# Token gate values computed behind the first expert step's activation, and the gate rows' difference taken by GpSimd

## The chip, the core and the metric

The kernel runs on one core of one Trainium2 chip. The core has TensorE (PE, matrix products and transposes), VectorE (DVE), ScalarE (ACT), GpSimd (POOL) and SyncE (SP, which here only starts transfers), each with an instruction list of its own; they meet through semaphores. 16 DMA engines serve all of the core's transfers. The metric is the device time of one execution in microseconds (us), the median of several.

## What is computed

Two layers of a backbone for 128 context tokens and 512 latent tokens of width 1024. Each layer normalises and modulates the rows, mixes them (pooling and attention), adds the result through a gate, and then runs a grouped mixture of 16 experts with two chosen for each token. The part that matters here, cut from the reference:

```python
def moe(h, router_w, router_b, w_gate, w_up, w_down):
    scores = jax.nn.sigmoid(t @ router_w)
    ...                                      # best group, then the top 2 in it: idx
    wts = jnp.take_along_axis(scores, idx, axis=-1)
    wts = wts / jnp.sum(wts, axis=-1, keepdims=True)
    gates = sum over the two of one_hot(idx) * wts
    act = jax.nn.silu(t @ w_gate) * (t @ w_up) * gates
    return act @ w_down

def trunk_layer(...):
    ...
    x = x + gate2 * moe(h2, ...)
```

`gates` are the token gates: two numbers for each token. `gate2` is a row of 1024 numbers, one row for context tokens and one for latent tokens.

## The kernel before

The kernel is written by hand in the order of each engine's list: one block of code per engine, no scheduler. Each engine runs its list in order; a wait holds all that stands behind it on that engine.

The expert stage of a layer works in steps of 128 gathered rows (`step(n, ...)` in the blocks of PE, ACT and DVE). Tokens are sorted by expert and padded to pieces of 32, so a step holds four tiles of 32 rows, of one to four experts. In this run the first layer has 12 steps and the second 13, numbered from 0. A step on PE (`products`, L1166) multiplies the rows by w_gate and w_up, in four pieces of weights; then `rest` turns the next step's rows (L1132), turns the activation (`turn_act`, L1176) and multiplies by w_down (L1193). In every step but the first of a layer, PE reads the weights of one tile from the ring directly, and ACT (L1499) and DVE (L2291) copy the weights of two others, six pieces a step, into buffers of their own (`part_copy_w`). DVE also multiplies the activation (L2335, two halves), copies half of the turned rows (L2240, `rows_copy`), makes the selected row of gate2 for each slot (L2346 and L2348, which read `is_ctx` and the difference of the two gate rows) and scales the step's output (L2361). ACT stores that output to `y_rows` in memory and then goes on to its next weight piece; the next step but one reads the buffer, so DVE waits for the store (`b_st`). All tensors that are views of one large buffer are called `big` or `actT` in the profile.

Ahead of the first step DVE works through the router: masks, sorted places, the list of rows for the gathers, the tables `fin` (how many steps until an expert is done), `eland` and `eslot` (which weights a tile needs). `r_fin` and `r_slot` tell the other engines that these are ready (L2253 and L2272). Then come the token gates (L2293 to L2304, ten instructions with a wait between most), and `r_gate` after them. The gates' result, `gates2`, is read first in step 2 (`early_gates`). In step 0, DVE takes the difference of the two gate rows (L2343), which L2348 reads in every step.

GpSimd issues the gathers of rows (L1681): the first and the second ahead of step 0, the others one by one as PE has turned the rows before (`b_t`). Each reads its list of rows from `idx`.

SP loads the experts' weights, three transfers of 1 MB each, into a ring of five buffers; `load_expert(e)` waits until the same part of expert e-1 has landed, and from expert 5 on until the buffer's last user is through. The router's scratch lies in the buffer that expert 3 gets. So SP holds the load of expert 3, and all behind it:

```python
                sp.wait_ge(r_gate, L(r_gate) + 1)
                sp.wait_ge(r_slot, L(r_slot) + 1)
                load_expert(3)
                load_expert(4)
```

Of the kernel before, what the change touches and what calls it, by code (L numbers as in the profile page):

```python
# [21 lines left out]
ALU = mybir.AluOpType  # L22
ACT = mybir.ActivationFunctionType
AX = mybir.AxisListType
# [129 lines left out]
def step_kernel(nc, x_prompt, x_sample, cache_ckv, cache_krope, c, c_ctx, ada_w, ada_b, norm1_g, norm2_g, w_in, pool_w,  # L154
# [3 lines left out]
    with es:  # L158
# [275 lines left out]
        def lsem(name, count):  # L434
# [29 lines left out]
        r_mask, r_tot, r_slot, r_fin = (lsem(n, 1) for n in (  # L464
            "r_mask", "r_tot", "r_slot", "r_fin"))
        c_x = lsem("c_x", NT)

        by_layer = [[sem(f"{n}{l}") for n in ("b_t", "b_ta", "b_td", "b_sil", "b_act", "b_at", "b_atc", "b_sel", "b_yd",
                                              "used", "b_st", "b_end", "w_a", "w_d")]
# [1086 lines left out]
        def _(pool):  # L1556
# [4 lines left out]
            for l in range(DEPTH):  # L1561
# [127 lines left out]
                gather(1)  # L1689
                pool.wait_ge(r_fin, L(r_fin) + 1)  # L1690
# [39 lines left out]
        def _(ve):  # L1730
# [69 lines left out]
            for l in range(DEPTH):  # L1800
# [492 lines left out]
                link(tt(gts, sig.rearrange("p (t g) k -> p t (g k)", g=EG), mask16[:, :, :], ALU.mult))  # L2293
                link(red(den, gts, AX.X, ALU.add))
                link(v.reciprocal(den, den))
                link(tt(gts, gts, bc(den, NE), ALU.mult))
                for w in range(2):
                    m = tt(hot[:, w], slot1, bc(pick[:, w, :], NE), ALU.is_equal)
                link(m)
                for w in range(2):  # L2300
                    m = tt(prod[:, w], hot[:, w], gts, ALU.mult)
                link(m)
                for w in range(2):
                    m = red(gates2[:, w * NT:(w + 1) * NT], prod[:, w], AX.X, ALU.add)  # L2304
                link(m)

                ve.sem_inc(r_gate, 1)
# [15 lines left out]
                def step(n, part, last):  # L2323
# [9 lines left out]
                    for k in range(2):  # L2333
                        cols = slice(k * P, (k + 1) * P)
                        v.tensor_tensor(act_n[:, cols], sil[:, cols], tb5[:, cols], ALU.mult).then_inc(b_act, 1)  # L2335
                    if not last:
                        rows_copy(n + 2)
                        if not part:
                            following = part_place(n + 1)
                        part_copy_w(n + 1, following, 0)  # L2340
                        if isinstance(n, int) and n == 0:
                            ve.wait_ge(ld_gate, 64 * l + 64)
                            link(tt(gate[:, 0, :], gate[:, 0, :], gate[:, 1, :], ALU.subtract))  # L2343
# [64 lines left out]
```

## Time and profile before

| | us |
|---|---|
| median of 3 runs | 1065.38 |
| lowest, highest | 1063.85, 1067.24 |
| the profiled execution | 1071.81 |
| its span | 1070.0 |

The profile is of one execution. A page gives each engine's busy time, 40 slices of the span (each digit is a busy share in tenths), and groups of instructions. Answers on the trace give instructions in order of time: start in us, duration in us (for several, from the first's start to the last's end), engine, line of the kernel, what is written and read, and in brackets the idle time before it on its engine with what ended that idle time. The first layer's expert stage runs from about 383 to 531 us, the second's from about 884 to 1050 us. Times in the text are counted from the span's start.

### The profile page before, as it was taken

What the parts mean: (1) busy time and instruction counts of PE and PEld (TensorE: products, weight loads), DVE (VectorE), ACT (ScalarE), POOL (GpSimd) and SP (SyncE); (2) the same over time, 40 slices, a digit from 0 to 9 for tenths busy, and PEclk for the clock granted to TensorE, in tenths of its full rate; (3) what the DMA queues carried; (4) which work ended last, traced back from release to release, by engine and by line L of the source; (5) the groups of instructions that cost most, each with busy time, mean ns of one, the idle gap of its engine ahead of it and who ended that gap; (6) DMA issues with size and microseconds to landing.
All of it is one profiled execution on the core that took longest, in us unless ns stands there. A gap on an engine that the chain in (4) does not pass through costs nothing.

```text
span 1070.0 us, 20675 instructions
## 1 busy us (share of the span) xinstructions
PE 1016.7 (95%) x7322; PEld 551.9 (52%) x7323; DVE 622.8 (58%) x1318; ACT 399.8 (37%) x810; POOL 205.9 (19%) x309
## 2 busy tenths in 40 slices
PE   3999999999999889999989999999999988999987
PEld 1566555555544454555456665555654435555442
DVE  0335455656535886666574545576734687776557
ACT  0332224444311126666433222444521114666550
POOL 0124358000000010010152435800000001000021
PEclk9999999999999999999999999999999999999998
DMA  9960005786800569999980000477250068999936
GB/s 349 373 181 1 1 0 205 276 310 248 332 21 38 197 270 408 419 419 417 374 297 6 1 0 1 185 290 284 86 212 20 40 221 357 420 418 417 411 136 252
DMA packets 71619, 237.90 MB, mean 222 GB/s; under 512 B 12192, under 2 KB 27568, under 8 KB 57216
## 3 DMA queue, kind: packets, MB, share of 16 engines
q1 hardware_dynamic: 59600, 195.36, 47.6%
q0 software_dynamic: 6480, 23.60, 6.0%
q10 hardware_dynamic: 5472, 18.12, 4.2%
q8 instruction: 34, 0.56, 0.2%
q14 instruction: 33, 0.27, 0.1%
HBM read 211.53 MB, written 25.53 MB: 222 GB/s over the span
## 4 chain that ended last, share of the span: by engine, by line
PE 81%; DVE 6%; DMA 5%; issue 3%; POOL 1%; SPq 1%; another core or an unknown queue 1%; ACT 1%; DVEq 0%; ACTq 0%; POOLq 0%
PE pair L1084 13%; PE bank L1166 13%; PE pair L801 8%; PE pair L1193 7%; PE pair L816 6%; PE pair L934 5%; PE bank L711 4%; PE pair L833 4%; PE bank L850 4%; PE bank L970 3%; PE bank L949 3%; DMA big<-ada_w 2%; PE pair L1132 2%; PE bank L785 2%; DMA y_rows<-big 1%
## 5 line engine op out<-in xcount | busy, mean ns | idle before, releaser
L1166 PE MATMUL bank<-big,actT 128*32 (+2 forms) x1168 | 178.6, 379 | 4.1 <-DVE big L2291 2.2
L1499 ACT ACTIVATE actT<-big 128x1024 f32 x138 | 144.3, 1055 | 71.7 <-PE bank L1166 27.0
L1166 PE MATMUL bank<-actT 128*32 128x256 f32 x1840 | 164.7, 379 | 0.0
L1084 PE MATMUL pair<-big,actT 128*128 128x512 f32 x320 | 142.7, 598 | 0.0
L1166 PEld LDWEIGHTS bank<-big,actT 128*32 128x32 f32 (+1 forms) x1168 | 98.9, 114 | 82.0 <-issue 23.7
L801 PE MATMUL pair<-big,actT 128*128 128x384 f32 (+1 forms) x320 | 95.1, 453 | 0.2 <-ACT actT L1256 0.2
L1084 PEld LDWEIGHTS pair<-big,actT 128*128 128x128 f32 x320 | 59.0, 190 | 67.8 <-issue 67.6
L1193 PE MATMUL pair<-big 128*32 (+2 forms) x384 | 92.9, 606 | 0.7 <-ACT big L1514 0.4
L2022 DVE TENSOR_REDUCE mx<-pair 128x1 f32<-128x640 f32 x64 | 52.7, 823 | 65.1 <-PE pair L935 65.0
L1166 PEld LDWEIGHTS bank<-actT 128*32 128x32 f32 x1840 | 86.3, 110 | 0.0
L1193 PE MATMUL pair<-actT,big 128*32 128x512 f32 x368 | 85.3, 607 | 0.0
L2291 DVE COPY big<-big 128x1024 f32 x92 | 63.5, 690 | 35.2 <-PE bank L1166 29.0
L1681 POOL DMA_INDIRECT big<-h_rows,big x25 | 29.8, 1190 | 259.3 <-PE pair L1132 226.9
L801 PEld LDWEIGHTS pair<-big,actT 128*128 128x128 f32 x320 | 60.6, 193 | 29.4 <-ACT actT L1256 1.7
L934 PE MATMUL pair<-big 96*128 96x512 f32 x128 | 70.7, 634 | 1.1 <-PE bank L711 0.9
L816 PE MATMUL pair<-actT,big 128*128 128x512 f32 (+1 forms) x256 | 70.9, 434 | 0.0
L1670 POOL TENSOR_SCALAR ss<-big 128x1 f32<-128x1 f32 x10 | 3.0, 302 | 339.0 <-ACT big L1441 339.0
L711 PE MATMUL bank<-big,condT 128*32 128x512 f32 x384 | 55.0, 657 | 13.6 <-DMA big<-ada_w 13.6
L1383 ACT ACTIVATE big<-pair,nmax 128x640 f32<-128x640 f32 x64 | 50.9, 795 | 18.9 <-DVE nmax L2025 18.5
L1441 ACT ACTIVATE big<-x 128x512 f32<-128x512 f32 x20 | 12.6, 630 | 115.9 <-DVE x L2162 115.9
L816 PEld LDWEIGHTS pair<-actT,big 128*128 128x128 f32 x256 | 39.1, 191 | 29.7 <-issue 29.7
L1193 PEld LDWEIGHTS pair<-big 128*32 128x32 f32 (+1 forms) x384 | 24.8, 114 | 50.5 <-issue 50.4
(303 smaller groups left out, 1627.8 us busy)
## 6 DMA issues: line engine op xcount, KB each, us to landing
big<-ada_w SPq DMA_DIRECT2D x48, 1024.0 KB, 6.3
big<-w_gate SPq DMA_DIRECT2D x32, 1024.0 KB
big<-w_up SPq DMA_DIRECT2D x32, 1024.0 KB
big<-w_down SPq DMA_DIRECT2D x32, 1024.0 KB
y_rows<-big ACTq DMA_DIRECT2D x24, 512.0 KB, 7.5
big<-w_out SPq DMA_DIRECT2D x4, 2048.0 KB, 10.1
big<-mod_rows SPq DMA_DIRECT2D x16, 512.0 KB, 7.0
h_rows<-big ACTq DMA_DIRECT2D x10, 512.0 KB, 2.7
```

The costliest lines, as they stand in the source:

```text
L711: m = mm(a7[32 * j:32 * j + 32, :], condT[:, k, :], w[:, j, :], start=(k == 0), stop=(k == DC - 1), tile_position=(0, 32 * j), skip_group_ ...
L801: m = mm(in_bank(t)[:, to:to + n], actT[:, k, t * P:(t + 1) * P], vw.win_q[:, k, lo:lo + n], start=(k == 0), stop=(k == DC - 1))
L816: m = mm(pair[0][:, to:to + cols], vw.win_p[:, k, g * P:(g + 1) * P], actT[:, k, t0:t0 + cols], start=(k == 0), stop=(k == DC - 1))
L833: m = mm(pair[1][:, n * HALF:n * HALF + 4 * QH], cqT[t % 2][:, k, :], vw.wuq[:, k, n * 4 * QH:(n + 1) * 4 * QH], start=(k == 0), stop=(k = ...
L934: mm(dst[:, 0:HALF], q, vw.kT[0:QH, h, 0:HALF], start=True, stop=True)
L1084: m = mm(dst, actT[:, k, t * P:(t + 1) * P], vw.wo[n][:, k, :], start=(k == order[0]), stop=(k == order[-1]))
L1166: m = mm(dst[lo:lo + m_, 0:DE], xgT[:, k, lo:lo + m_], weights(c, k % 4 * DE, DE), start=(k == 0), stop=(k == DC - 1), tile_position=(0, l ...
L1193: m = mm(pair[1][lo:lo + m_, j * HALF:(j + 1) * HALF], acT[:, k, lo:lo + m_], weights(c, j * HALF, HALF), start=(k == 0), stop=(k == 1), t ...
L1383: f(prob[un % 4][:, :, :], score_bank(un)[:, 0:NLK * P].rearrange("p (k n) -> p k n", n=P), ACT.Exp, bias=nmax[:, un % 2:un % 2 + 1], scal ...
L1499: f(parts[1][i % 3], slot[:, i * PIECE:(i + 1) * PIECE], ACT.Copy).then_inc(w_a, 1)
L2022: link(v.tensor_reduce(mx[:, un % 2:un % 2 + 1], score_bank(un)[:, 0:NLK * P], AX.X, ALU.max))
L2291: v.tensor_copy(parts[2][i % 3], slot[:, i * PIECE:(i + 1) * PIECE]).then_inc(w_d, 1)
```

## The change

The token gates become a function, `token_gates`, that DVE calls in step 0, behind the two activation products and ahead of the copy of the turned rows; before, they stood ahead of step 0. With them goes the signal `r_gate`. The difference of the gate rows is computed by GpSimd, between the second gather and the wait for `r_fin`, and signalled by a new semaphore `g_diff`, on which DVE waits in step 0 at the place where it computed the difference. The last layer's `b_end`, which nobody uses, is not made.

```diff
@@ GpSimd
                 gather(1)
+                pool.wait_ge(ld_gate, 64 * l + 64)
+                tt(gate[:, 0, :], gate[:, 0, :], gate[:, 1, :], ALU.subtract).then_inc(g_diff, 1)
                 pool.wait_ge(r_fin, L(r_fin) + 1)
@@ DVE
-                link(tt(gts, sig.rearrange("p (t g) k -> p t (g k)", g=EG), mask16[:, :, :], ALU.mult))
...
-                link(m)
-
-                ve.sem_inc(r_gate, 1)
+                def token_gates():
+
+                    link(tt(gts, sig.rearrange("p (t g) k -> p t (g k)", g=EG), mask16[:, :, :], ALU.mult))
...
+                    link(m)
+                    ve.sem_inc(r_gate, 1)
+
@@ DVE, step(n, part, last)
                         v.tensor_tensor(act_n[:, cols], sil[:, cols], tb5[:, cols], ALU.mult).then_inc(b_act, 1)
+                    if isinstance(n, int) and n == 0:
+                        token_gates()
                     if not last:
                         rows_copy(n + 2)
                         if not part:
                             following = part_place(n + 1)
                         part_copy_w(n + 1, following, 0)
                         if isinstance(n, int) and n == 0:
-                            ve.wait_ge(ld_gate, 64 * l + 64)
-                            link(tt(gate[:, 0, :], gate[:, 0, :], gate[:, 1, :], ALU.subtract))
+                            ve.wait_ge(g_diff, L(g_diff) + 1)
```

On DVE, at the end of the first layer's router and the start of step 0, the list before (lines L2293 to L2304 are the token gates, L2335 the activation products; a name in brackets is a semaphore that the instruction waits for):

```order
467 L2272 TENSOR_SCALAR big<-big 128x57 [waits dve_chain]
468 L2293 TENSOR_TENSOR big<-big,mask 128x80 [waits r_fin,r_slot]
469 L2294 TENSOR_REDUCE big<-big 128x5 [waits dve_chain]
470 L2295 RECIPROCAL big<-big 128x5 [waits dve_chain]
471 L2296 TENSOR_TENSOR big<-big 128x80 [waits dve_chain]
472 L2298 TENSOR_TENSOR big<-big 128x80 [waits dve_chain]
473 L2298 TENSOR_TENSOR big<-big 128x80
474 L2301 TENSOR_TENSOR big<-big 128x80 [waits dve_chain]
475 L2301 TENSOR_TENSOR big<-big 128x80
476 L2304 TENSOR_REDUCE gates<-big 128x5 [waits dve_chain]
477 L2304 TENSOR_REDUCE gates<-big 128x5
478 L2335 TENSOR_TENSOR big<-big,bank 128x128 [waits dve_chain,used0,b_sil0]
```

The same place on DVE after the change (L2339 is the activation product, L2297 to L2308 the gates, L2242 the copy of the turned rows):

```order
467 L2274 TENSOR_SCALAR big<-big 128x57 [waits dve_chain]
468 L2339 TENSOR_TENSOR big<-big,bank 128x128 [waits b_sil0,used0,r_fin,r_slot]
469 L2339 TENSOR_TENSOR big<-big,bank 128x128
470 L2297 TENSOR_TENSOR big<-big,mask 128x80
471 L2298 TENSOR_REDUCE big<-big 128x5 [waits dve_chain]
...
478 L2308 TENSOR_REDUCE gates<-big 128x5 [waits dve_chain]
479 L2308 TENSOR_REDUCE gates<-big 128x5
480 L2242 COPY actT<-pair 128x512 [waits dve_chain,b_t0]
```

The gates have moved behind both activation products, and so behind what these wait for: PE's products (`used0`) and ACT (`b_sil0`).

On GpSimd, around the second gather (the DMA rows; `TENSOR_LOAD fin` reads the number of steps), before:

```order
136 L1681 DMA big<-h_rows,big 128x1024 [waits r_idx,h_st1,h_st0]
137 L1681 DMA big<-h_rows,big 128x1024 [waits b_t0,r_idx]
138 L1691 TENSOR_LOAD fin [waits r_fin]
139 L1691 ISA x2
140 L1681 DMA big<-h_rows,big 128x1024 [waits b_t0] x8
```

and after:

```order
136 L1681 DMA big<-h_rows,big 128x1024 [waits r_idx,h_st1,h_st0]
137 L1681 DMA big<-h_rows,big 128x1024 [waits b_t0,r_idx]
138 L1691 TENSOR_TENSOR big<-big 128x1024 [waits ld_gate]
139 L1693 TENSOR_LOAD fin [waits r_fin]
140 L1693 ISA x2
141 L1681 DMA big<-h_rows,big 128x1024 [waits b_t0] x8
```

One operation on 1024 columns is added behind the second gather's issue. SP's list is the same before and after; expert 3's first load is the one that waits for `r_gate`:

```order
64 L639 DMA big<-w_down 128x2x1024 [waits ld_wd]
65 L629 DMA big<-w_gate 128x2048 [waits r_slot,ld_wg,r_gate,op_x]
66 L634 DMA big<-w_up 128x2048 [waits ld_wu]
67 L639 DMA big<-w_down 128x2x1024 [waits ld_wd]
68 L629 DMA big<-w_gate 128x2048 [waits ld_wg]
```

Nothing moved in it; what it waits for is now signalled from another place in DVE's list.

## Rows read from the trace of the kernel before

**Rows 1.** The page: busy time by engine, and DMA's busy share in 40 slices.

```profile
PE 1016.7 (95%) x7322; PEld 551.9 (52%) x7323; DVE 622.8 (58%) x1318; ACT 399.8 (37%) x810; POOL 205.9 (19%) x309
...
DMA  9960005786800569999980000477250068999936
```

**Rows 2.** DVE in order of time, first layer: start, duration, line, [idle before it].

```profile
386.50 0.17 DVE L2248 TENSOR_SCALAR fin<-big 128x16 int32<-128x16 f32 x1
...
387.09 0.18 DVE L2253 TENSOR_TENSOR actT<-actT 128x19 f32<-128x19 f32 x1
...
389.97 0.24 DVE L2293 TENSOR_TENSOR big<-big,mask 128x80 f32<-128x80 f32 x1
...
391.88 0.38 DVE L2304 TENSOR_REDUCE gates<-big 128x5 f32<-128x80 f32 x2
392.48 0.49 DVE L2335 TENSOR_TENSOR big<-big,bank 128x128 f32<-128x128 f32 x2 [0.23 <-DVE gates L2304]
393.85 0.69 DVE L2240 COPY actT<-pair 128x512 f32<-128x512 f32 x1 [0.88 <-PE pair L1132]
...
396.21 1.22 DVE L2343 TENSOR_TENSOR big<-big 128x1024 f32<-128x1024 f32 x1
```

**Rows 3.** PE in order of time, at the stages' starts and in step 10.

```profile
383.61 7.14 PE L1166 MATMUL bank<-big,actT 128*128 128x256 f32 x32 [0.36 <-issue]
392.25 0.55 PE L1132 MATMUL pair<-cst,big 128*128 128x128 f32 x3 [1.50 <-DMA big<-h_rows,big]
...
399.79 0.40 PE L1166 MATMUL bank<-big,actT 128*32 x1 [0.64 <-DVE big L2291]
...
511.97 0.39 PE L1166 MATMUL bank<-actT 128*32 128x256 f32 x3
...
893.46 0.33 PE L1176 MATMUL bank<-cst,big 128*128 128x128 f32 x1 [0.72 <-DVE big L2335]
...
900.49 0.40 PE L1166 MATMUL bank<-big,actT 128*32 x1 [0.71 <-DVE big L2291]
...
1013.24 0.40 PE L1166 MATMUL bank<-big,actT 128*32 x1 [0.70 <-ACT actT L1499]
```

**Rows 4.** SP's queue in order of time: loads of w_gate.

```profile
392.38 0.33 SPq L629 DMA_DIRECT2D big<-w_gate  x1
...
504.56 0.33 SPq L629 DMA_DIRECT2D big<-w_gate  x1
...
893.04 0.33 SPq L629 DMA_DIRECT2D big<-w_gate  x1
```

**Rows 5.** Stretches: engines' busy us, PE clock, DMA share, GB/s at the end.

```profile
392.00:393.00 1.00, 0.72 (x5) 0.48 (x6) 0.74 (x4) 0.00 (x0) 0.00 (x0) 1.00 0.00 0
410.00:450.00 40.00, 39.19 (x574) 20.36 (x574) 28.88 (x52) 25.00 (x32) 3.52 (x3) 1.00 1.02 419
```

**Rows 6.** DVE and ACT in order of time: weight copies around step 10.

```profile
504.72 0.69 DVE L2291 COPY actT<-big 128x1024 f32 x1 [0.59 <-DMA big<-w_gate]
...
1005.94 0.69 DVE L2291 COPY actT<-big 128x1024 f32 x1 [2.01 <-DMA big<-w_gate]
...
510.74 1.06 ACT L1499 ACTIVATE actT<-big 128x1024 f32 x1 [2.55 <-PE bank L1166]
...
1012.04 1.06 ACT L1499 ACTIVATE actT<-big 128x1024 f32 x1 [4.05 <-issue]
```

**Rows 7.** GpSimd and DVE in order of time, where both are at work.

```profile
167.30 1.33 POOL L1616 TENSOR_TENSOR big<-big 128x687 f32<-128x687 f32 x1 [0.17 <-POOL big L1628]
...
167.89 0.77 DVE L2011 TENSOR_SCALAR nmax_c<-mx_c 128x4 f32<-128x4 f32 x1
...
383.86 1.97 POOL L1681 DMA_INDIRECT big<-h_rows,big  x1 [5.82 <-DVE big L2244]
```

**Rows 8.** GpSimd's groups by line and shape: count, busy us, mean ns.

```profile
L1628 POOL TENSOR_TENSOR big<-big 128x656 f32<-128x656 f32 x8 | 12.6, 1576 | 0.7
```

**Rows 9.** DVE in order of time, last step of the second layer.

```profile
1043.40 0.48 DVE L2335 TENSOR_TENSOR big<-big,bank 128x128 f32<-128x128 f32 x2 [4.93 <-remote]
```

More of the change, by code:

```diff
@@ L463, in step_kernel @@
         op_mm, op_g, op_x = (lsem(n, 2 * NT) for n in ("op_mm", "op_g", "op_x"))
-        r_mask, r_tot, r_slot, r_fin = (lsem(n, 1) for n in (
-            "r_mask", "r_tot", "r_slot", "r_fin"))
+        r_mask, r_tot, r_slot, r_fin, g_diff = (lsem(n, 1) for n in (
+            "r_mask", "r_tot", "r_slot", "r_fin", "g_diff"))
         c_x = lsem("c_x", NT)
-        by_layer = [[sem(f"{n}{l}") for n in ("b_t", "b_ta", "b_td", "b_sil", "b_act", "b_at", "b_atc", "b_sel", "b_yd",
-                                              "used", "b_st", "b_end", "w_a", "w_d")]
+        by_layer = [[sem(f"{n}{l}") if n != "b_end" or l + 1 < DEPTH else None for n in (
+            "b_t", "b_ta", "b_td", "b_sil", "b_act", "b_at", "b_atc", "b_sel", "b_yd", "used", "b_st", "b_end", "w_a", "w_d")]
                     for l in range(DEPTH)]
@@ L2291, in part_copy_w @@
                     v.tensor_copy(parts[2][i % 3], slot[:, i * PIECE:(i + 1) * PIECE]).then_inc(w_d, 1)
-                link(tt(gts, sig.rearrange("p (t g) k -> p t (g k)", g=EG), mask16[:, :, :], ALU.mult))
[L2294 to L2298, printed above, removed]
-                link(m)
[L2300 to L2305, printed above, removed]
-                ve.sem_inc(r_gate, 1)
+                def token_gates():
+                    link(tt(gts, sig.rearrange("p (t g) k -> p t (g k)", g=EG), mask16[:, :, :], ALU.mult))
+                    link(red(den, gts, AX.X, ALU.add))
+                    link(v.reciprocal(den, den))
+                    link(tt(gts, gts, bc(den, NE), ALU.mult))
+                    for w in range(2):
+                        m = tt(hot[:, w], slot1, bc(pick[:, w, :], NE), ALU.is_equal)
+                    link(m)
+                    for w in range(2):
+                        m = tt(prod[:, w], hot[:, w], gts, ALU.mult)
+                    link(m)
+                    for w in range(2):
+                        m = red(gates2[:, w * NT:(w + 1) * NT], prod[:, w], AX.X, ALU.add)
+                    link(m)
+                    ve.sem_inc(r_gate, 1)
                 def early_gates():
```

## Prediction

> **What bounds the kernel now.** I read the page first: TensorE (PE) is busy for 95% of the span, and the row of DMA shares stands at 9 through both expert stages [rows 1]. So two resources are nearly full there at once, PE and the 16 DMA engines, and a change in front of these stages must be read against both. The reader is then to follow, in the first layer, the end of the routing. DVE's list of the router ends with the gate values, 389.97 to 392.26 (391.88 + 0.38), then come the two activation products at 392.48 [rows 2]. PE had ended the first step's products at 390.75 (383.61 + 7.14) and was waiting for the gathered rows, which came at 392.25 [rows 3]. So in this layer the gates cost PE nothing at that point. In the second layer PE waited 0.72 us for the same DVE line, at 893.46 [rows 3]. Next, 3.7 us into DVE's step, the difference of the gate rows (L2343) takes 1.22 us [rows 2], and behind it PE stands for 0.64 us in one layer and 0.71 us in the other, each time until DVE's copy of the next weight piece [rows 3]. These are what the change can take away on PE: at most 0.64, and 0.72 + 0.71.
>
> The second thing to see is the weight stream. SP holds the loads of expert 3 and of all later ones behind r_gate, because expert 3's buffer covers the router's scratch. They start at 392.38 and 893.04, 0.12 us after the last gate value in the first layer [rows 2, 4]. In 392 to 393 DMA moves nothing [rows 5]: expert 2 has landed, and only r_gate keeps the queue empty. From then on it is full: 1.02 of its share, 419 GB/s, from 410 to 450, and 9 in all slices to the end of the stage [rows 1, 5]. A queue that is full from its first byte to its last cannot make good a late start. The question is then whether any consumer waits for it. One does, in the step numbered 10 of either layer: DVE waits for w_gate at 504.72 for 0.59 us and at 1005.94 for 2.01 us [rows 6]. SP's own list confirms the landing: in the first layer it sends the next w_gate, which waits for the one before to land, at 504.56 [rows 4].
>
> **Gate values moved behind the activation.** No instruction is added, ten small ones lie later (from the first multiply to the two reductions, 2.29 us in all). DVE can now multiply the activation when PE is through: 390.75, 0.14 us to hand over (ScalarE's copy ends at 1013.10, PE goes on at 1013.24 [rows 3, 6]), 0.49 us for both halves [rows 2], so the gates begin at 391.38 in place of 389.97. That is 1.4 us later, and r_gate with them. What is queued behind this on SP is expert 3's three loads and everything after. What is queued behind on DVE is its copy of the turned rows: the gates would end at 393.67, and before that copy started at 393.85 [rows 2], so here the cover holds, with 0.2 us to spare. PE gains up to 0.7 us at this point in the second layer alone.
>
> **Difference of the gate rows on GpSimd.** It leaves DVE's list (1.22 us, twice) and stands on GpSimd between the issue of the second gather and the wait for r_fin. The issue ends at 385.83 (383.86 + 1.97) [rows 7], the gate rows have landed long before, and the value is needed where L2346 follows, some 10 us later; the new wait on g_diff should find it ready, and the third gather, behind it on GpSimd, is not due before PE has turned the rows of the second, which it begins at 392.25 [rows 3]. Its length is in no row. The nearest are GpSimd's own element-wise operations: 1.33 us for 687 columns of an addition [rows 7], so 1.98 us for 1024, and 1.577 us for 656 columns of L1628 [rows 8], so 2.46 us. I take 2.46 us, since L1628 too is a subtraction that writes over an input. It ends at 388.29.
>
> The cost of this is what it does to DVE. At 167.30 GpSimd runs a 1.33 us operation; a DVE operation on four columns, started at 167.89, ends at 168.66, three hundredths after GpSimd is done, and took 0.77 us where small ones take 0.17 [rows 2, 7]. So a DVE operation can be held until GpSimd's is over. In the new place the subtraction runs from 385.83, and DVE's next tensor-scalar operation is L2248 at 386.50 [rows 2]. Held until 388.29 it loses 1.8 us, and the whole list behind it with it. Bounds: 0 if nothing is held, 2.0 us if GpSimd starts after a gap of 0.2 us. I take 1.8 us, since the row that shows the holding is of the same kind as L2248.
> The Trainium skill ("SBUF — State Buffer", Who interferes with whom) says that the later of two such operations waits for the whole of the other. It counts a DVE operation as such where it has two inputs in SBUF, or runs in a mode that takes both ports. L2248 writes integers and may not be in that mode; by the rule the first surely held is then a two-input one, L2253 at 387.09 [rows 2], 0.6 us further down the list. The sum would then be 1.2 us smaller. The row at 167.89 has a single wide input and was held, so the trace speaks for the larger figure.
>
> With DVE 1.8 us late, the activation is multiplied at 391.77 (389.97 + 1.8), is over at 392.26, and the gates begin 2.3 us later than before (392.26 against 389.97). r_gate, the loads of experts 3 to 15, and their landings move by 2.3 us in each layer. PE still finds the activation at about the time at which its first transposes of the gathered rows are done. The copy of the turned rows moves from 393.85 to about 394.8, and of the 1.22 us saved on DVE's list some 0.3 us is left when PE comes to the next weight piece. This small gain on PE does not last, as the next sum shows.
>
> **Where it lands.** In step 10 DVE's copy of w_gate follows the landing. Behind it in order stand the selection, the next copy and the scaling of the expert's output; then ScalarE stores that output and only then, 6.0 us after DVE's copy began, copies its own next piece (504.72 to 510.74, and 1005.94 to 1012.04, 6.1 us) [rows 6]. In the second layer PE stands 0.70 us for exactly this piece at 1013.24 [rows 3]. In the first ScalarE's copy ends at 511.80 and PE takes the piece at 511.97 [rows 3, 6]; with 0.14 us to hand over it has 0.03 us to spare. So both layers have no slack there, and whatever PE gained earlier it waits away: PE's place after this step is the landing plus a constant. The terms are 2.3 - 0.03 in the first layer and 2.3 in the second, together **4.6 us**. The profiled execution took 1071.81 us, so it would take 1076.4. The median of the runs shown is 6.43 us lower; I carry the microseconds over: 1065.38 + 4.6 = **1070.0 us**, 0.43% slower.
>
> **Rivals.**
> (a) GpSimd does not hold DVE back. Then r_gate is late by the 1.4 us of the moved gates alone, and the sum is 2 x 1.4 = 2.8 us: 1068.2, within 0.3%. For it speaks that I have no row of L2248's own kind beside GpSimd; against it the row at 167.89.
> (b) The weights are in time after all. The margin in step 10 was read from one execution; where DMA runs ahead by some 2 us more against PE in the runs that are timed, the late start is hidden, and the gains on PE stay: 0.64 + 1.22 (the second layer's two waits together, limited by what leaves DVE's list), so 1.9 us faster, 1063.5. This is how the change ends on the other side; the point from which it decides is a landing about 2 us earlier than the two rows show. Against it: 2.01 us of DVE waiting in the second layer [rows 6].
> (c) A wait at the end moves. In the last step DVE starts its activation product only at 1043.40 after 4.93 us idle, its releaser not named in the records [rows 9]; after PE's products it should be 0.14 us. If this is DVE's code coming in late, two instructions fewer in its list may move it to where it hides, worth up to 3.9 us: 4.6 - 3.9 = 0.7, so 1066.1.
> The Trainium skill ("Runtime: NRT & Kernel Launch", Instruction fetch mechanics) says that code comes in blocks of 256 instructions, each engine by its own queue. By that, two instructions can move such a stall only if it sits on a block's edge, which no row here shows.
> (d) The late weights meet a second place as well, such as the copies for step 2, and PE loses more than DMA's delay: some 2 us more, 1072.
>
> **How the numbers follow.** A difference of 0.3% (3.2 us) is about what a measurement of this kernel can tell from no change. Chances: forecast 0.50, (a) 0.20, (b) 0.12, (c) 0.10, (d) 0.08. The range goes from between (b) and (c), 1064.8, to just short of (d), 1071.8, and leaves out most of (b) and (d). Slower by over 0.3%, above 1068.6: most of the forecast (0.43), a little of (a) (0.05), all of (d), so 0.56. Faster, under 1062.2: a part of (b), 0.07. The rest, 0.37, is within.
>
> **What the profile after would show.** The gates' multiply after the activation product and not before it; SP's first load of expert 3 near 394.7 and 895.3 rather than 392.4 and 893.0, with DMA idle until then; L2248 held until GpSimd's subtraction ends, or not, which separates the forecast from (a); PE's stop at the second weight piece of step 1 shorter; and in step 10 DVE's wait for w_gate longer, with PE's stop behind ScalarE's copy about 3 us in the second layer and over 2 us in the first. If DVE does not wait for w_gate in step 10, the prediction is wrong and (b) holds. If the loads start no later, my reading of r_gate is wrong.

## The result, and the profile after the change

| | us |
|---|---|
| before, median of 21 runs | 1065.97 (1062.63 to 1070.86) |
| changed, median of 21 runs | 1070.33 (1067.76 to 1074.71) |
| changed / before | 1.0041, 95% interval 1.0030 to 1.0053 |
| profiled execution of the changed kernel, its span | 1074.35, 1072.5 |

The change costs 4.4 us (0.41% of 1065.97; 3.2 to 5.6). The prediction was 1070.0, 4.6 us slower.

First the end of the routing in the first layer. Columns are as before: start, duration, engine, line, operation, and in brackets the idle time with what ended it. Lines lie lower by a few numbers (L2248 is now L2250, the gates L2293 to L2304 are L2297 to L2308, L2291 is L2293, L2272 is L2274). In order of the engines PE, GpSimd, DVE, SP:

```profile
384.86 7.14 PE L1166 MATMUL bank<-big,actT 128*128 128x256 f32 x32 [0.59 <-ACT actT L1483]
...
387.10 2.36 POOL L1691 TENSOR_TENSOR big<-big 128x1024 f32<-128x1024 f32 x1
...
387.74 1.76 DVE L2250 TENSOR_SCALAR fin<-big 128x16 int32<-128x16 f32 x1
...
392.79 0.48 DVE L2339 TENSOR_TENSOR big<-big,bank 128x128 f32<-128x128 f32 x2
...
395.09 0.38 DVE L2308 TENSOR_REDUCE gates<-big 128x5 f32<-128x80 f32 x2
...
395.59 0.33 SPq L629 DMA_DIRECT2D big<-w_gate  x1
```

GpSimd's subtraction takes 2.36 us. The DVE operation that starts inside it, on 16 columns, takes 1.76 us where it took 0.17 [rows 2], and ends within 0.04 us of it: it was held, for 1.6 us. The activation is multiplied behind that, then come the gates, and 0.12 us after the last of them SP sends expert 3's first load. To compare the two executions I count from the start of the first products, since this execution came to the place 1.25 us later (384.86 against 383.61 [rows 3]): the load is sent 10.73 us behind it, before it was 8.77 (392.38 [rows 4] less 383.61). So it is **1.96 us later**. In the second layer it is 10.78 against 8.80:

```profile
886.67 7.14 PE L1166 MATMUL bank<-big,actT 128*128 128x256 f32 x32 [0.59 <-ACT actT L1483]
...
895.28 0.54 PE L1132 MATMUL pair<-cst,big 128*128 128x128 f32 x3 [1.47 <-DVE big L2274]
...
897.45 0.33 SPq L629 DMA_DIRECT2D big<-w_gate  x1
```

The middle row is a wait that I had not foreseen: PE needs `r_slot` (DVE's L2274) before it goes on behind the first products, and DVE, held by GpSimd, is late with it. (The experiment e4_drained_after below shows that it is so in the first layer too.)

The windows show DMA at 0.00 for three whole microseconds where before it was so for one [rows 5] (columns: stretch, length, busy time and count of PE, PEld, DVE, ACT and POOL, granted clock, DMA share, GB/s):

```profile
392.00:393.00 1.00, 0.00 (x1) 0.00 (x0) 0.82 (x5) 0.00 (x0) 0.00 (x0) 1.00 0.19 74
393.00:394.00 1.00, 0.35 (x3) 0.36 (x4) 0.90 (x6) 0.00 (x0) 0.00 (x0) 1.00 0.00 0
394.00:395.00 1.00, 1.00 (x10) 0.99 (x9) 0.93 (x5) 0.56 (x3) 0.00 (x0) 1.00 0.00 0
395.00:396.00 1.00, 1.00 (x3) 0.41 (x3) 0.81 (x4) 0.59 (x1) 0.77 (x1) 1.00 0.00 0
```

And where the late loads meet a consumer, DVE's copies of weights and PE behind them: the first layer in step 2 and step 10, then the second layer in step 10.

```profile
412.98 0.69 DVE L2293 COPY actT<-big 128x1024 f32 x1 [5.07 <-DMA big<-w_gate]
...
413.93 0.40 PE L1166 MATMUL bank<-big,actT 128*32 x1 [2.91 <-DVE actT L2293]
...
508.24 0.69 DVE L2293 COPY actT<-big 128x1024 f32 x1 [1.15 <-DMA big<-w_gate]
...
515.46 0.40 PE L1166 MATMUL bank<-big,actT 128*32 x1 [0.34 <-ACT actT L1499]
...
1010.15 0.69 DVE L2293 COPY actT<-big 128x1024 f32 x1 [4.33 <-DMA big<-w_gate]
...
1011.09 0.40 PE L1166 MATMUL bank<-big,actT 128*32 x1 [2.44 <-DVE actT L2293]
```

DVE's waits in step 10 have grown from 0.59 to 1.15 us and from 2.01 to 4.33 us [rows 6]. But in the first layer PE's loss comes far earlier, in step 2, where it stands for 2.91 us.

### The profile page after: what moved, and what is told of

The parts are those of the page before. It is cut to its first block, busy times and chain, and to the rows that moved or that the text cites. A ratio compares the mean times of both kernels' runs of the same rounds, so it can differ in the third digit from the quotient of the medians.

```text
span 1072.5 us, 20675 instructions
## 1 busy us (share of the span) xinstructions
PE 1017.8 (95%) x7322; PEld 552.7 (52%) x7323; DVE 623.1 (58%) x1316; ACT 399.1 (37%) x810; POOL 210.7 (20%) x311
## 4 chain that ended last, share of the span: by engine, by line
PE 77%; DMA 10%; DVE 4%; SPq 3%; issue 3%; POOL 2%; ACT 1%; DVEq 0%; POOLq 0%; ACTq 0%
PE pair L1084 13%; PE bank L1166 9%; PE pair L801 7%; PE pair L816 6%; PE pair L1193 6%; PE pair L934 6%; DMA big<-w_gate 4%; PE bank L711 4%; PE pair L833 4%; PE bank L850 4%; PE bank L970 3%; PE bank L949 3%; DMA big<-w_down 2%; PE bank L785 2%; PE pair L1132 2%
## 5 line engine op out<-in xcount | busy, mean ns | idle before, releaser
L2293 DVE COPY big<-big 128x1024 f32 x92 | 63.4, 689 | 33.8 <-PE bank L1166 26.0
```

Source lines behind the costliest of these rows:

```text
L2293: v.tensor_copy(parts[2][i % 3], slot[:, i * PIECE:(i + 1) * PIECE]).then_inc(w_d, 1)
```

## The experiments

Theory L is the prediction's: the time follows the start of expert 3's loads. All runs but the last look at before are compared with runs of the kernel before on the same chip, made between them. A cost in us is the ratio's excess times the median of before in that comparison. The ratio on record is not the quotient of the two medians given beside it; the two differ by up to 0.1 per cent (in e2_pool_diff 1.0039 and 1.0049), and the intervals belong to the ratio. Rivals B and C are those of the expectations, not (b) and (c) of the prediction.

### The gates alone

```diff
@@ against the changed kernel, GpSimd
-                pool.wait_ge(ld_gate, 64 * l + 64)
-                tt(gate[:, 0, :], gate[:, 0, :], gate[:, 1, :], ALU.subtract).then_inc(g_diff, 1)
@@ DVE, step 0
-                            ve.wait_ge(g_diff, L(g_diff) + 1)
+                            ve.wait_ge(ld_gate, 64 * l + 64)
+                            link(tt(gate[:, 0, :], gate[:, 0, :], gate[:, 1, :], ALU.subtract))
```

> The changed kernel with the difference of the gate rows back on DVE, at its old place in step 0; only the token gates are moved. Theory L (the late start of the loads is the whole cost): r_gate comes 1.4 us later in each layer, so the loads of expert 3 start near 393.8 and 894.4, DVE's wait for w_gate in step 10 grows by as much, and the kernel takes 2.8 us more than before (ratio 1.0026). Rival B (GpSimd's hold of DVE is what costs, and the gates alone are free or help): within 1 us of before, or up to 0.7 us faster. In both GpSimd has no element-wise work there and L2250 takes 0.17 us.

Measured: 1070.02 us against 1066.12, ratio 1.0032 (1.0015 to 1.0049), so 3.4 us more. The loads are sent 1.3 us later than before, counted from the products (394.07 - 383.98 = 10.09, and 895.81 - 885.70 = 10.11). Rival B is out: moving the gates alone costs, and GpSimd has no part in it.

### The difference on GpSimd alone

```diff
@@ against the changed kernel, DVE: token_gates() is called here and not in step 0
+                token_gates()
+
                 def early_gates():
...
-                    if isinstance(n, int) and n == 0:
-                        token_gates()
```

> The changed kernel with the token gates back ahead of step 0; only the difference of the gate rows is on GpSimd. Theory L: DVE is held for 1.6 us at L2250 (measured in the changed kernel: 1.76 and 1.75 us against 0.17), r_gate and the loads come 1.6 us later in each layer, step 10 waits longer, 3.2 us more than before (ratio 1.0030). PE waits longer for the first activation product too, 1.6 us and 2.3 us, and both are inside the same shift. Rival B (late weights are covered; what counts is DVE's list in step 0): 1.6 us lost and 1.22 us saved on it in each layer, so 0.8 us more (1.0008).

Measured: 1071.38 against 1066.12, ratio 1.0039 (1.0018 to 1.0061), 4.2 us more. The rows are DVE's held operation and, in both layers, PE's wait for the activation product (L2341 here), which is new in the first layer and was 0.72 us in the second [rows 3]:

```profile
387.10 1.77 DVE L2250 TENSOR_SCALAR fin<-big 128x16 int32<-128x16 f32 x1
...
395.00 0.47 PE L1176 MATMUL bank<-cst,big 128*128 128x128 f32 x1 [1.46 <-DVE big L2341]
...
896.51 0.48 PE L1176 MATMUL bank<-cst,big 128*128 128x128 f32 x1 [1.63 <-DVE big L2341]
```

In the kernel of the gates alone the same DVE operation took 0.17 us. So the hold is GpSimd's doing. The Trainium skill ("SBUF — State Buffer", Who interferes with whom) lets a DVE operation with one SBUF input be blocked only in a mode that uses both port pairs, and I had doubted that one that writes integers is in such a mode. Ten rows of it beside the subtraction, in the five kernels that have it on GpSimd, show 1.75 to 1.77 us: this form was blocked each time.

Each half of the change costs nearly as much as the whole (3.4 and 4.2 against 4.4). By delays of the loads it should be so only in part: 2.6 and 3.2 us against 3.9, both layers together. The halves do not add up since, with the gates alone moved, DVE stands idle for PE's products before it turns to the activation and the gates (its line is L2337 there); 0.96 us in the first layer, 0.95 in the second; in the changed kernel the hold falls into that idle time. The intervals are too wide to say more of the sizes.

### The signal alone, by two amounts

The kernel before, and `r_gate` is signalled later. No other instruction moves.

```diff
@@ DVE
                 link(m)

-                ve.sem_inc(r_gate, 1)
@@ e3_signal_late, step 0
                         rows_copy(n + 2)
+                        if isinstance(n, int) and n == 0:
+                            ve.sem_inc(r_gate, 1)
@@ e11_signal_later, step 0, in place of that, behind the selected gate row (b_sel)
+                    if isinstance(n, int) and n == 0:
+                        ve.sem_inc(r_gate, 1)
```

> The kernel before with a single move: the signal r_gate is given behind the copy of the turned rows in step 0 rather than behind the last gate value. No instruction of any engine takes longer or starts later but SP's loads. Theory L: the signal comes 2.1 us later (392.26 to about 394.4), the loads start near 394.5 and 895.1, step 10 waits 2.1 us longer in each layer, the kernel takes 4.2 us more (ratio 1.0039). Rival B (the loads have slack, DVE's list is what counts): no change, within 0.5 us.

Measured: 1070.98 against 1066.12, ratio 1.0035 (1.0018 to 1.0052), 3.7 us more. **This is the run that decides.** No instruction of an engine is moved or made longer, only the loads are later, and that costs 3.7 of the change's 4.4 us, for a delay of 2.8 us against 3.9. The signal came 0.1 us behind the start of the copy (the first row below) and not at its end, so the loads are 1.4 us later, not 2.1 (393.88 - 383.70 = 10.18, 894.11 - 883.93 = 10.18). In the first layer they are missed at the place where the changed kernel misses them:

```profile
393.78 0.69 DVE L2240 COPY actT<-pair 128x512 f32<-128x512 f32 x1 [0.93 <-PE pair L1132]
...
393.88 0.33 SPq L629 DMA_DIRECT2D big<-w_gate  x1
...
411.12 0.69 DVE L2291 COPY actT<-big 128x1024 f32 x1 [3.69 <-DMA big<-w_gate]
...
412.06 0.40 PE L1166 MATMUL bank<-big,actT 128*32 x1 [1.54 <-DVE actT L2291]
```

> The kernel of e3_signal_late with the signal r_gate given still later in step 0, behind the selection of the gate row (near 397.7): SP's loads of expert 3 start 5.3 us later than before in each layer, and nothing else changes. Theory L (DMA is full from its first byte of expert 3 to step 10, so the time goes up by the delay, layer by layer): 10.6 us more, ratio 1.010. Between e3 (1.4 us a layer, 3.7 us measured) and this one the slope is then one to one. Rival C (e3 and the changed kernel lost some 4 us by another cause that a later signal doesn't raise): within 2 us of e3, ratio 1.003 to 1.005.

Measured: 1075.94 against 1068.08, ratio 1.0090 (1.0058 to 1.0122), 9.6 us more, for loads that are 5.2 us later in each layer (10.4 us together).

```profile
397.32 0.33 SPq L629 DMA_DIRECT2D big<-w_gate  x1
...
414.38 0.69 DVE L2291 COPY actT<-big 128x1024 f32 x1 [7.44 <-DMA big<-w_gate]
...
415.32 0.63 PE L1166 MATMUL bank<-big,actT 128*32 x1 [4.98 <-DVE actT L2291]
```

Again step 2. Rival C falls: the cost rises with the delay.

But the profile doesn't divide this cost as theory L has it. From the start of the first products to the end of the last w_down product, the first layer takes 154.7 us, against 148.3 in the second look at before (147.1 in the first): 6.4 us more for loads that are 5.2 us later. The second layer takes 164.1 against 161.3, so 2.8 us more for the same delay. One part of the first layer's loss is not the delay at all. Behind PE's stop of 4.98 us the granted clock lay at half, the 1.2 GHz level, until 421:

```profile
413.00:414.00 1.00, 0.00 (x0) 0.00 (x0) 0.00 (x0) 0.00 (x0) 0.00 (x0) 1.00 1.03 430
...
415.00:416.00 1.00, 0.68 (x8) 0.41 (x12) 0.96 (x3) 0.00 (x0) 0.00 (x0) 0.50 1.02 422
...
420.00:421.00 1.00, 1.00 (x16) 0.55 (x12) 0.00 (x0) 0.17 (x1) 0.00 (x0) 0.50 0.98 410
```

From its restart to the first w_down product of step 2, PE needs 11.3 us here (415.32 to 426.65) and 8.9 us in the changed kernel, at full clock (413.93 to 422.79). By this estimate 2.5 of the 9.6 us are the clock's. Two executions of one kernel differ by over a microsecond here (147.1 and 148.3), so the division is rough, but that the sum comes near the delay is in part luck.

### The loads no longer behind the signal

The router's scratch lies only in the columns of expert 3's w_down. So w_gate and w_up of expert 3 can go ahead of `r_gate`.

```diff
@@ SP, against the changed kernel
-                def load_expert(e):
+                def load_expert(e, held=None):
...
+                    if held is not None:
+                        sp.wait_ge(held, L(held) + 1)
                     sp.dma_start(wd[s][:, :, :], ...
...
-                sp.wait_ge(r_gate, L(r_gate) + 1)
+                load_expert(3, held=r_gate)
                 sp.wait_ge(r_slot, L(r_slot) + 1)
-                load_expert(3)
```

> The changed kernel, in which only the third transfer of expert 3 (w_down, whose columns are the ones that the router's scratch lies in) waits for r_gate; w_gate and w_up of expert 3 go out as soon as expert 2's have landed. The moved gates and GpSimd's difference stay. Theory L: DMA has no gap behind expert 2, SP's third transfer near 395 queues behind 2 MB that are under way and comes in time, so all 4.6 us of the change are gone and its gains on PE appear: 0.64 us in the first layer, up to 1.2 us in the second, and the 0.7 us of step 10 in the second; 2 to 2.5 us under before (ratio about 0.998). Rival B: still 4 us above before (1.004), because DVE is as late as it was.

Measured: 1065.99 against 1066.12, ratio 0.9996 (0.9979 to 1.0013). The cost of the change is gone, with moved gates and GpSimd's hold still there: rival B's 4 us are excluded. But the further gain of 2 us doesn't show (the interval of the ratio reaches from 2.2 us under before to 1.4 over). PE's rows tell where it could go:

```profile
394.73 0.62 PE L1133 MATMUL pair<-cst,big 128*128 128x128 f32 x3 [3.35 <-DMA big<-h_rows,big]
...
893.62 0.90 PE L1133 MATMUL pair<-cst,big 128*128 128x128 f32 x3 [2.55 <-DMA big<-h_rows,big]
```

PE stands for the second gather 3.35 and 2.55 us, against 1.50 [rows 3] and 0.81 us before, 3.6 us more in both layers. The gather needed 10.2 us to land in the first layer (the DMA issues of this stretch, with the median time to landing), 9.4 us in the second; before, it needed 8.3 and 7.7 us, and PE had its rows 8.39 us after the issue began (392.25 - 383.86 [rows 3, 7]).

```profile
big<-h_rows,big POOLq DMA_INDIRECT x1, 10.2
```

Behind that stop the granted clock was at half, the 1.2 GHz level, for some three microseconds (0.54, 0.50, 0.50 from 395 to 398), and in the second layer, around the end of the 2.55 us, for about as long:

```profile
394.00:395.00 1.00, 0.27 (x2) 0.27 (x3) 0.78 (x5) 0.00 (x0) 0.00 (x0) 1.00 1.09 459
395.00:396.00 1.00, 1.00 (x7) 1.00 (x6) 0.00 (x0) 0.28 (x1) 0.00 (x0) 0.54 0.84 352
396.00:397.00 1.00, 1.00 (x5) 0.98 (x5) 0.11 (x1) 0.39 (x2) 0.00 (x0) 0.50 0.83 176
...
894.00:895.00 1.00, 1.00 (x7) 1.00 (x6) 0.52 (x3) 0.22 (x1) 0.00 (x0) 0.50 1.06 442
895.00:896.00 1.00, 1.00 (x6) 1.00 (x5) 0.00 (x0) 0.33 (x2) 0.00 (x0) 0.50 0.95 401
```

### Loads early, but not beside the gather

Three kernels with one more line on SP: expert 3's w_gate waits until expert 2's w_down has landed.

```diff
@@ SP, against the split above
+                sp.wait_ge(ld_wd, landed(l, 2))
                 load_expert(3, held=r_gate)
```

> The kernel of e5_split_after with one more wait on SP: w_gate of expert 3 goes out only when expert 2's w_down has landed (near 391.7), and w_down of expert 3 still waits for r_gate. So at no time do more transfers stand beside the second gather of rows than in the kernel before. In e5_split_after PE stood 3.35 and 2.55 us for that gather against 1.50 and 0.81 us before. Theory L with contention (the gather shares the DMA queues with expert 3's early loads, and that ate the gain of e5): PE's wait for the gather returns to about 1.6 us, DMA has no gap, step 10 has no wait, and the time is 2 to 2.5 us under before (ratio 0.998). Rival (PE's wait there comes from DVE or GpSimd being late, not from contention): the wait stays near 3 us and the ratio at 1.000, as e5.

Measured: 1065.36 against 1066.41, ratio 0.9996 (0.9979 to 1.0012). PE's stop ahead of the second rows is back at 1.66 and 1.64 us, and the gather lands 7.9 and 8.5 us after its issue, where it took 10.2 and 9.4. But the stop of the first layer is not the gather's, though the profile names it:

```profile
384.56 1.97 POOL L1683 DMA_INDIRECT big<-h_rows,big  x1 [6.46 <-DVE big L2248]
...
392.03 0.19 DVE L2276 TENSOR_SCALAR big<-big 128x57 int32<-128x57 int32 x1
...
393.12 0.54 PE L1134 MATMUL pair<-cst,big 128*128 128x128 f32 x3 [1.66 <-DMA big<-h_rows,big]
```

The rows had landed at about 392.5 (384.56 + 7.9), and PE went on 0.7 us later; where it does wait for the gather, it goes on within 0.1 us of the landing (in e5_split_after 384.49 + 10.2 = 394.69 and 394.73). It went on 0.90 us behind DVE's L2276, which signals `r_slot`; PE's list waits for that signal, then loads the number of steps, and only then turns the rows. The same 0.9 us lie between the two in the first layer of the changed kernel, of e2_pool_diff and of e9_two_deep_after. So wherever GpSimd holds DVE, `r_slot` keeps PE for 1.65 us at the least there, however early the rows come.

The gain of 2 us is again not shown (the interval reaches from 2.2 us under before to 1.3 over). Here the start explains it: expert 3's load is sent 0.8 and 0.2 us earlier than before, counted from the products (392.28 - 384.31, 890.61 - 881.99), no more, since the signal that expert 2 has landed comes only then. And step 10 of the second layer waits as it did before:

```profile
1003.53 0.69 DVE L2295 COPY actT<-big 128x1024 f32 x1 [2.07 <-DMA big<-w_gate]
```

What PE gains in steps 0 and 1 it gives back at the weights.

> The kernel before with the same new order on SP as e4_drained_after: w_gate of expert 3 when expert 2 has landed, its w_down after r_gate. The loads start about 0.7 us earlier than before and the gap in DMA (392 to 393) goes. Theory L: only the waits for weights in step 10 can shrink, 0.7 us on PE in the second layer and nothing in the first, so 0.5 to 0.7 us under before, ratio 0.9994. If the loads had more to give than step 10 shows: over 2 us under before (0.998).

Measured: 1066.41 against 1066.41, ratio 1.0001 (0.9980 to 1.0021). The loads start 0.1 us later and 0.7 us earlier than before. The forecast of 0.5 to 0.7 us of gain is too small for this interval; nothing is shown either way.

> The kernel of e1_gates_moved (gates behind the activation, difference of the gate rows on DVE) with the order of e4_drained_after on SP. Theory L: the moved gates no longer delay any load; PE's 0.72 us before the first activation of the second layer goes and its 0.7 us in step 10 of that layer too, while DVE's 1.22 us for the difference stays in the path to the second weight piece: 1.4 us under before, ratio 0.9987. Against e4_drained_after it says what GpSimd's part is worth once the loads are in time: by the theory 1 us less gain than e4.

Measured: 1068.13 against 1066.41, ratio 1.0005 (0.9981 to 1.0030). The loads start 0.1 and 0.3 us earlier. The forecast of 1.4 us of gain lies inside the interval, as zero does; it isn't confirmed.

### Two transfers under way in place of three

```diff
@@ SP, load_expert, against the split above
+                    if e == 3:
+                        sp.wait_ge(ld_wu, landed(l, 2))
                     if e > 0:
                         sp.wait_ge(ld_wg, landed(l, e - 1))
...
+                    if e == 3:
+                        sp.wait_ge(ld_wd, landed(l, 2))
                     if e > 0:
                         sp.wait_ge(ld_wu, landed(l, e - 1))
...
+                    if e == 2:
+                        sp.wait_ge(ld_wg, landed(l, 2))
                     if held is not None:
```

> The changed kernel with early loads for expert 3 as in e5_split_after, but from expert 2's w_down to expert 3's w_up SP keeps two transfers under way and not three: each goes out when the last but one has landed. Expert 3's w_down waits for r_gate as in e5. Theory: the second gather of rows shares DMA with whatever stands beside it, so it lands sooner than in e4_drained_after (PE waits under 1 us for it, against 1.66 and 1.64), while DMA keeps full and the loads run some 2 us or more further ahead than in e4. So both limits on PE move, at the gather and in step 10, and the kernel is 2 to 4 us under before: ratio 0.997. Rival (the gather is slow for another reason than the transfers beside it): PE still waits 1.6 to 3 us there, and the ratio is 0.999 to 1.000.

Measured: 1064.72 against 1068.08, ratio 0.9974 (0.9954 to 0.9995), 2.8 us under before. It beats both kernels. But PE's stop ahead of the second rows did not get shorter (1.65 and 1.48 us), and the second layer names why:

```profile
893.31 0.54 PE L1139 MATMUL pair<-cst,big 128*128 128x128 f32 x3 [1.48 <-DVE big L2281]
```

It is `r_slot` again (L2281 here), late by GpSimd's hold of DVE. In the first layer too: the rows had landed at 391.5, and PE went on at 392.14, 0.89 us behind L2281.

> The same order on SP as e9_two_deep_after, on the kernel of e1_gates_moved: the difference of the gate rows stays on DVE. Theory: against e9 DVE has 1.22 us more in step 0 and PE about 0.7 us more to wait at the second weight piece, but DVE is not held for 1.6 us by GpSimd ahead of the activation, which matters once the gathered rows come early. So within 1 us of e9, ratio 0.997 to 0.998. If GpSimd's hold doesn't matter, it is 1.2 to 1.5 us behind e9.

Measured: 1066.02 against 1068.08, ratio 0.9982 (0.9965 to 0.9999). Without the hold PE's stop does get shorter, 0.29 us in the first layer and 0.75 in the second:

```profile
391.54 0.55 PE L1139 MATMUL pair<-cst,big 128*128 128x128 f32 x3 [0.29 <-DMA big<-h_rows,big]
...
400.20 0.40 PE L1173 MATMUL bank<-big,actT 128*32 x1 [1.34 <-DVE big L2298]
```

What is won there, PE waits two stages on for DVE's weight piece, behind the difference that DVE still computes.

> The kernel before with the order on SP of e9_two_deep_after: two transfers under way from expert 2's w_down on, expert 3's w_gate and w_up early, its w_down after r_gate. Gates and difference stay where they were before. It says which part of the gain of e9 (0.9974 of before) and e10 (0.9982) is the new order of the loads alone. If the order alone does it: 0.998, that is 2 us under before. If the moved gates are needed for it, because the activation product then ends PE's wait in place of the gather: PE waits 1.4 to 2 us for DVE's activation product in both layers, and the time is within 1 us of before, 0.999 to 1.001. I expect the second more than the first, since in the kernel before the first activation product began at 392.48, only 0.2 us after the gathered rows came.

Measured: 1064.89 against 1066.86, ratio 0.9982 (0.9965 to 1.0000). My expectation missed: PE waits 0.73 and 0.96 us for the activation, not 1.4 to 2, and the time is about 2 us under before with the order of the loads alone, though the interval just reaches no gain at all. The three kernels, 0.9974, 0.9982 and 0.9982, can't be told apart. So the gain goes with the order of the loads, and no run shows one from the moved gates or the difference on GpSimd.

### The kernel before once more

> The kernel before, unchanged, profiled a second time. Its first profile has 4.93 us of DVE idle without a named releaser ahead of the last activation product (1043.40), and a time 5.8 us over the median. If that stall sits at a fixed place of DVE's code, it is here again, as long. If it is a chance of that one execution, it is not here, PE waits under 0.5 us for that product, and the time is 1064 to 1068.

Measured: 1069.06 us in one run, a little over the range I gave. The stall ahead of the last activation product [rows 9] isn't there: DVE was idle 1.06 us, PE 0.41. The first of the rows is PE's stop in the first profile, the others are of the second:

```profile
1043.74 0.69 PE L1176 MATMUL bank<-cst,big 128*128 128x128 f32 x2 [4.28 <-DVE big L2335]
...
1039.60 0.48 DVE L2335 TENSOR_TENSOR big<-big,bank 128x128 f32<-128x128 f32 x2 [1.06 <-PE bank L1166]
...
1039.95 0.53 PE L1176 MATMUL bank<-cst,big 128*128 128x128 f32 x2 [0.41 <-DVE big L2335]
...
407.38 0.69 DVE L2291 COPY actT<-big 128x1024 f32 x1 [1.63 <-DMA big<-w_gate]
```

So the 4.93 us were a matter of one execution. They cost more than their length: PE stood for 3.9 us longer (4.28 less 0.41), and behind that, with the granted clock at 0.50 from 1042 to 1048, it needed 6.6 us to the end of w_down (1043.74 to 1050.33) in place of 4.5 (1039.95 to 1044.48). Together these are 5.9 us, about the 5.8 by which the first profiled execution lies above the median of 21 runs. The second has a pause of its own without a named releaser, 2.51 us on PE in step 1 of the second layer (908.54). The last row shows something that the first profile hid: in step 2 of the unchanged kernel DVE does wait for w_gate.

## Why the prediction was right, point by point

The kernels whose loads of expert 3 follow a single start, in order of that start. The delay is the send of its first load less the start of the first products, both layers together, less 17.57 us, which is the same sum for before (8.77 + 8.80).

| kernel | loads later, us | time over before, us (95%) |
|---|---|---|
| e4_drained_after | -1.0 | -0.4 (-2.2 to 1.3) |
| e6_drained_before | -0.7 | 0.1 (-2.1 to 2.2) |
| e7_drained_gates | -0.4 | 0.5 (-2.0 to 3.2) |
| e1_gates_moved | 2.6 | 3.4 (1.6 to 5.2) |
| e3_signal_late | 2.8 | 3.7 (1.9 to 5.5) |
| e2_pool_diff | 3.2 | 4.2 (1.9 to 6.5) |
| the change | 3.9 | 4.4 (3.2 to 5.6) |
| e11_signal_later | 10.4 | 9.6 (6.2 to 13.0) |

Each of the eight intervals holds the delay itself, so a cost of one for one fits seven edits of different kinds and the change. The first three can't be told from zero. The last fits in part by luck: by its profile the first layer lost more than its delay, the clock's 2.5 us among it, and the second less. What is shown is that a later start alone costs time, and more of it the later it is; how near to one for one it stays over ten microseconds is not.

- **Gates moved, 1.4 us later**: right. Alone they make it 1.3 us. The new order on DVE is as described.
- **GpSimd's subtraction, 2.46 us, holds DVE for 1.8 us**: right in kind, somewhat large. It took 2.36 us and held for 1.6. The row at 167.89 [rows 7] was the right one to go by. Rival (a) is out.
- **Loads 2.3 us later in each layer**: mis-sized by 0.35 us. It was 1.96 and 1.98, of which the hold's smaller size is 0.2.
- **No slack, so the delay becomes time**: right in kind, shown by the signal alone and its second amount; one for one is what the intervals allow. The sum by the measured delay is 3.9 us; 4.6 came nearer to the measured 4.4 than the step's own size warrants, and the interval holds both.
- **The place, step 10 of both layers**: half wrong. In the second layer it is step 10 (2.44 us on PE at DVE's piece, 0.53 at a later one, where I had named ScalarE's). In the first it is step 2, with 2.91 us, and step 10 has 0.34 left. The step that failed is the search for consumers without margin: I took those that already waited in one profile. In step 2 the same profile had w_gate landing at about the moment of DVE's copy, with nothing to spare, and SP's own list told it:

```profile
408.61 0.33 SPq L629 DMA_DIRECT2D big<-w_gate  x1
...
408.68 0.69 DVE L2291 COPY actT<-big 128x1024 f32 x1 [1.30 <-PE pair L1193]
```

SP sends the next w_gate when the last has landed, 408.61; DVE copies at 408.68. Rival (d) named this place but wanted 2 us on top. There is no such sum: what PE loses in step 2 it doesn't lose in step 10, since either only ties it to the same stream of loads.

- **The small gains on PE**: PE's stop at the second weight piece of step 1 is gone in the first layer (0.64 us [rows 3]) and 0.17 us in the second (0.71 [rows 3]). As foreseen, it brought nothing. With the loads in time (e4) it brought nothing that can be told from zero either.
- **PE's wait for `r_slot`** was missing in my list of what a late DVE holds. In the changed kernel it costs nothing on top, as PE is tied to the loads later on; with the loads early it takes the place of the wait for the gather (e9, and the first layer of e4).
- **Rival (c)**: the profiled stall was no fixed property of the code. The changed kernel had none there (PE waited 0.41 us), and the unchanged one had none the second time. DVE's idle time there is 1.06 us without it, not the 0.14 that the prediction gave. The Trainium skill ("Runtime: NRT & Kernel Launch", Instruction fetch mechanics) says that code comes in blocks of 256 instructions; by that I would look for such a stall at the same instruction each time, and the second profile doesn't have it there. What it was stays open.
- **The carry from the profiled execution to the median**: it held because only the difference was carried over. The two profiled executions differ by 2.5 us, the medians by 4.4. The one before contained the stall and lies 5.8 us above its median, the changed one lies 4.0 above its own, and why is not known.

Open is why the gather lands later beside more loads. The Trainium skill ("DMA: Bandwidth & Descriptors", Queues, rings and completion order) has each DMA engine take turns between queues, a packet from each; by that alone, more transfers waiting in SP's one queue would not slow GpSimd's. The landings here go the other way. In e5 two more megabytes were sent in that time and the gather landed after 10.2 and 9.4 us; in the kernel before (both looks), the changed one, e2, e3 and e4 it took 7.3 to 8.5 us; with two transfers under way (e9, e10, e12) 7.1 to 7.9. No run here tells the number of the transfers under way from the bytes that are sent.

## What to carry to other kernels

Find the queue that is full from its first byte to its last, and cost every edit by what it does to that queue's start: here a signal that "only" comes later cost 3.7 of the whole change's 4.4 us. Look for a consumer's margin by comparing landing times with the times of use, also where nothing waits yet; a wait of zero is no slack. And when small instructions are moved behind the critical work, look at each signal that moves with them: the part of a buffer that the scratch doesn't cover can be loaded without it.

## What was not expected of the hardware

- PE's pauses of 3.35 and 2.55 us for the gather were followed by some three microseconds at half the granted clock. In those of 4.28 us (the first look at before, at its end) and 4.98 us (e11) it fell within the pause and stayed there for about five and six microseconds behind it. Behind the pauses of 1.65, 2.91 and 2.44 us in the changed kernel, and of 2.51 us in the second look at before, it stayed at 1.00. So the length of one pause doesn't tell it alone: 2.55 us was followed by the half level, 2.91 us was not.
- A semaphore signalled by an instruction of its own behind a DVE copy reached SP when the copy began, not when it ended: in e3_signal_late DVE's copy ran from 393.78 for 0.69 us, and SP sent its load at 393.88; in the second layer the copy began at 893.99 and the load went at 894.11.
- One profiled execution of a kernel can hold a stall of 5 us that a second does not, and by the clock behind it the stall cost 5.9 us.
